# First expert block's rows from one-hot products instead of a gather, and half of its weights split earlier

## What is computed

```python
h2 = modulate(rmsnorm(x, norm_ffn[l]), sh2, sc2)
x = x + gt2[:, None, :] * moe(h2, ...)

def moe(h, router_w, router_bias, w_gate, w_up, w_down):
    scores = jax.nn.sigmoid(jnp.einsum('bsd,de->bse', h, router_w))
    sel = scores + router_bias
    grp = lax.top_k(sel.reshape(B, S, N_GROUPS, per), TOP_K)[0].sum(-1)
    g_idx = jnp.argmax(grp, axis=-1)
    ...
    _, e_idx = lax.top_k(jnp.where(in_grp, sel, -jnp.inf), TOP_K)
    w = jnp.take_along_axis(scores, e_idx, axis=-1)
    w = w / jnp.sum(w, axis=-1, keepdims=True)
    hid = silu(h @ w_gate[e]) * (h @ w_up[e])      # for each chosen expert e
    return sum over chosen e of w[e] * (hid @ w_down[e])
```

## Time and profile before

| what | us |
|---|---|
| median of 3 runs | 2239.13 |
| lowest and highest of these | 2235.25, 2240.95 |
| the profiled execution's own time | 2234.31 |
| its span, from the first to the last instruction | 2232.5 |
| TensorE's granted clock over that span, share of full speed | 0.989 |

### The profile page before, as it was taken

The page is one execution under the profiler, slowest core; times in us unless marked ns, Lnnn a source line. Parts: engine busy times, 40 slices in busy tenths (PEclk is TensorE's granted clock), DMA queues, the critical chain, the costliest instruction groups (busy, mean ns, idle before and its releaser), DMA issues.

```text
span 2232.5 us, 32746 instructions
## 1 busy us (share of the span) xinstructions
PE 2124.1 (95%) x12051; PEld 1703.5 (76%) x12051; DVE 1484.5 (66%) x2695; ACT 1010.4 (45%) x1867; POOL 381.1 (17%) x346
## 2 busy tenths in 40 slices
PE   7999999999899999999999999999998999999996
PEld 4897788787687786777679978888966878677774
DVE  4728766655767876777646487666367688377775
ACT  4523334554565325555435333345445643445551
POOL 2002200000001431444300021000000034124441
PEclk9999999999999999999999999999999999999998
DMA  9332233241325765766542222333222277446653
GB/s 315 95 88 62 81 119 95 77 120 55 89 93 183 267 240 222 276 250 248 189 150 88 81 81 85 102 110 105 77 70 81 81 257 270 201 158 240 244 211 121
DMA packets 196573, 333.71 MB, mean 149 GB/s; under 512 B 30528, under 2 KB 153280, under 8 KB 180416
## 3 DMA queue, kind: packets, MB, share of 16 engines
q1 hardware_dynamic: 169184, 305.33, 40.4%
q0 software_dynamic: 19296, 19.98, 2.8%
q10 hardware_dynamic: 7936, 6.30, 0.9%
HBM read 352.48 MB, written 51.38 MB: 181 GB/s over the span
## 4 chain that ended last, share of the span: by engine, by line
PE 76%; DVE 12%; ACT 5%; issue 3%; DMA 2%; POOL 0%; SPq 0%; POOLq 0%; DVEq 0%; ACTq 0%
PE ps L875 70%; PE ps L873 6%; DVE spare L2089 3%; DVE ring_rounded L2107 2%; ACT WH_rounded L1588 1%; DMA SQKV<-gate_logits 1%; DVE nmax L2344 1%; DVE SC L2717 1%; DMA Y<-y_rows 1%; DVE ps L2341 0%; DVE ssq L2274 0%; POOL M L3059 0%; DVE SC L2367 0%; DVE spare L2092 0%; DVE SQKV L2285 0%
## 5 line engine op out<-in xcount | busy, mean ns | idle before, releaser
L875 PE MATMUL ps<-X_rounded,WH_rounded 128*128 128x512 f32 x768 | 340.0, 443 | 16.4 <-DVE ring_rounded L2107 4.5
L2107 DVE TENSOR_TENSOR ring_rounded<-ring,WH_rounded 128x512 fp32r<-128x512 f32 (+2 forms) x190 | 234.6, 1243 | 132.8 <-ACT WH_rounded L1588 132.4
L875 PE MATMUL ps<-H_rounded,WH_rounded 128*128 128x512 f32 x768 | 301.4, 392 | 3.2 <-DVE SC L2717 3.0
L875 PE MATMUL ps<-X_rounded,ring_rounded 128*128 128x512 f32 x768 | 301.7, 393 | 0.0
L875 PE MATMUL ps<-WH_rounded,X_rounded 128*128 128x256 f32 (+1 forms) x960 | 274.8, 286 | 3.1 <-ACT TM L1800 1.0
L875 PE MATMUL ps<-ring_rounded,X_rounded 128*128 128x256 f32 (+1 forms) x960 | 271.3, 283 | 0.0
L875 PE MATMUL ps<-WH_rounded,H_rounded 128*128 128x256 f32 (+1 forms) x960 | 271.2, 282 | 0.0
L3059 POOL TENSOR_TENSOR M<-M,SC 128x512 f32<-128x512 f32 x48 | 79.5, 1670 | 947.0 <-DVE SC L2717 947.0
L1588 ACT ACTIVATE WH_rounded<-ring 128x512 fp32r<-128x512 f32 (+2 forms) x190 | 195.1, 1036 | 77.0 <-PE ps L875 65.5
L875 PEld LDWEIGHTS ps<-X_rounded,WH_rounded 128*128 128x128 f32 x768 | 144.9, 189 | 69.4 <-issue 27.9
L875 PEld LDWEIGHTS ps<-WH_rounded,X_rounded 128*128 128x128 f32 x960 | 184.4, 192 | 5.3 <-issue 2.4
(11 more groups left out here) (399 smaller groups left out, 4484.0 us busy)
## 6 DMA issues: line engine op xcount, KB each, us to landing
ring<-in_w_in SPq DMA_DIRECT2D x272, 256.0 KB, 4.0
Y<-in_moe_w_down SPq DMA_DIRECT2D x18, 1024.0 KB, 6.8
ring<-in_ada_w SPq DMA_DIRECT2D x64, 256.0 KB, 4.6
ring<-in_w_branch SPq DMA_DIRECT2D x64, 256.0 KB, 5.3
TM<-in_ada_w SPq DMA_DIRECT2D x14, 1024.0 KB, 10.0
DQK<-in_ada_w SPq DMA_DIRECT2D x14, 1024.0 KB, 9.2
ring<-in_moe_w_down SPq DMA_DIRECT2D x14, 1024.0 KB, 5.9
gate_logits<-CM SPq DMA_DIRECT2D x44, 256.0 KB, 2.7
```

Source lines behind the costliest of these rows:

```text
L875: ins = nc.tensor.matmul(o, lhsT, rhs, start=start, stop=stop)
L2107: ins = v.tensor_tensor(low[j][:, at:at + size], ring[:, j, at:at + size], high[i][:, at:at + size].bitcast(F32), ALU.subtract)
```

## The change

**Rows of block 0.** DVE makes four one-hot tiles first_hot (128 tokens by 128 places each, in CM) as soon as it has the ranks: the place's number is compared with the token's rank in expert 0, times whether the token chose it. PE multiplies the token rows h_tok with these, 32 products of 128 columns (two halves, four feature tiles each, summed over four token tiles), straight into banks 2 and 0, where rows_turn(0) put its result. This goes ahead of the find products. gather(0), rows_turn(0) and their place in rows_in go; gather(1) is the first, and gather(2), which writes over h_tok's first tile, waits for rows_used[0], which PE gives behind the products. The stores of h to DRAM stay, as the other blocks are gathered.

**Weights of block 0.** The first two quarters of pair_high(0) go ahead of the sigmoid on ACT, with the wait for the two weight loads; the first two of pair_low(0) go ahead of the router's steps on DVE. The other two quarters stay where all four were. DVE's turn_low(0) now also waits for h_stored, since it writes over a tile of h_tok.

**Products that nobody reads.** warm(13) becomes warm(4); warm(8) and warm(2) go.

```diff
--- before.py
+++ after.py
@@ -549,6 +549,7 @@
...
         onehot = heads(sc[:, 0:2 * S], 2 * NT)
+        first_hot = heads(flat(CM[:, :, :])[:, 2 * S:3 * S], NT)
...
@@ -1438,8 +1439,22 @@
...
                 free(1)
-                warm(13, 5)
+                warm(4, 5)
+                eng.wait_ge(h_copied, p.next(h_copied, 2))
+                alone()
+                for b in (0, 2):
+                    free(b)
+                    alone()
                 eng.wait_ge(routed, p.next(routed, 2))
+                for f in range(2):
+                    for k in range(4):
+                        for t in range(NT):
+                            last = (k, t) == (3, NT - 1)
+                            ins = mm(ps[:, (2, 0)[f], tt(k)], h_tok[t][:, 4 * f + k::NC], first_hot[:, t],
+                                     t == 0, t == NT - 1, last=last)
+                    ins.then_inc(turned[f], p.gives(turned[f]))
+                later(rows_used[0])
+                eng.wait_ge(routed, p.next(routed))
...
                 alone()
                 for n in range(2 * NT):
@@ -1448,15 +1463,13 @@
...
-                eng.wait_ge(h_copied, p.next(h_copied, 2))
-                for b in (0, 1, 3, 4, 5, 6, 7):
+                for b in (1, 3, 4, 5, 6, 7):
...
                     alone()
                 for c in range(NC):
...
-                warm(8, 5)
...
                 def rows_turn(j):
...
@@ -1513,8 +1526,6 @@
...
                     later(expert_used)
...
-                rows_turn(0)
-                warm(2, 5)
                 for j in range(BLOCKS + 1):
...
@@ -1967,6 +1978,24 @@
                 shift(3 * NC, Hc, h_ready)
                 nc.scalar.preload_act_table_set("sigmoid_and_others")
...
+                def pair_high(j, qs=range(4)):
+                    if 0 in qs and SEQ[j] < NE:
+                        for m in range(2):
+                            at = (3 * j + m) % SLOTS
+                            eng.wait_ge(place_loaded[at], p.next(place_loaded[at], 16))
+                    elif 0 in qs:
+                        eng.wait_ge(over_loaded[j % AHEAD], p.next(over_loaded[j % AHEAD], 48))
+                    for q in qs:
+                        act(piece(pair_hi[j % 2], q), piece(pair_w[j % AHEAD], q), ACT.Copy).then_inc(
+                            act_high, p.gives(act_high))
+                for i in (0, 1):
+                    p.mark(place_loaded[i], 16 * (l == 0))
+                for i in ROW_PLACES:
+                    p.mark(place_loaded[i], 16)
+                pair_high(0, range(2))
                 eng.wait_ge(filled[6], p.next(filled[6]))
                 act(scores_T, ps[0:NE, 6], ACT.Sigmoid).then_inc(emptied[6], p.gives(emptied[6]))
...
@@ -1990,23 +2019,7 @@
...
-                def pair_high(j):
-                    if SEQ[j] < NE:
-                        for m in range(2):
-                            at = (3 * j + m) % SLOTS
-                            eng.wait_ge(place_loaded[at], p.next(place_loaded[at], 16))
-                    else:
-                        eng.wait_ge(over_loaded[j % AHEAD], p.next(over_loaded[j % AHEAD], 48))
-                    for q in range(4):
-                        act(piece(pair_hi[j % 2], q), piece(pair_w[j % AHEAD], q), ACT.Copy).then_inc(
-                            act_high, p.gives(act_high))
-                for i in (0, 1):
-                    p.mark(place_loaded[i], 16 * (l == 0))
-                for i in ROW_PLACES:
-                    p.mark(place_loaded[i], 16)
-                pair_high(0)
+                pair_high(0, range(2, 4))
                 turn_copy(0)
                 for j in range(BLOCKS + 1):
...
@@ -2024,7 +2037,7 @@
...
                 eng.wait_ge(routed, p.next(routed, 2))
-                p.mark(routed, 3)
+                p.mark(routed, 4)
...
@@ -2761,6 +2774,16 @@
...
                 p.mark(filled[7])
+                def pair_low(j, qs=range(4)):
+                    for q in qs:
+                        eng.wait_ge(act_high, p.next(act_high))
+                        v.tensor_tensor(piece(pair_lo[j % AHEAD], q), piece(pair_w[j % AHEAD], q),
+                                        piece(pair_hi[j % 2], q).bitcast(F32), ALU.subtract).then_inc(
+                            act_ready, p.gives(act_ready))
+                pair_low(0, range(2))
                 eng.wait_ge(handed[7], p.next(handed[7]))
...
@@ -2842,6 +2865,10 @@
...
                 rank, n_of, extra, upto, first = place_of[:, 1], *(counts[:, k] for k in range(4))
                 eng.wait_ge(emptied[0], p.given(emptied[0]))
+                for t in range(NT):
+                    ins = v.tensor_scalar(first_hot[:, t], iota[:, :], rank[:, t * NE:t * NE + 1],
+                                          whole[:, 0, t * NE:t * NE + 1], ALU.is_equal, ALU.mult)
+                ins.then_inc(routed, p.gives(routed))
                 past, beyond = whole[:, 1], whole[:, 2]
...
@@ -2890,22 +2917,19 @@
...
                 def turn_low(j):
...
+                    if j == 0:
+                        eng.wait_ge(h_stored, p.next(h_stored, 16 * NT))
+                        alone()
+                        eng.wait_ge(act_high, p.next(act_high, 2))
                     for f in range(2):
                         at = slice(4 * f, 4 * f + 4)
-                        eng.wait_ge(act_high, p.next(act_high))
+                        if j:
+                            eng.wait_ge(act_high, p.next(act_high))
                         v.tensor_tensor(rows_lo[j % 2][:, at], bank3((2, 0)[f], 4, P),
...
-                def pair_low(j):
-                    for q in range(4):
-                        eng.wait_ge(act_high, p.next(act_high))
-                        v.tensor_tensor(piece(pair_lo[j % AHEAD], q), piece(pair_w[j % AHEAD], q),
-                                        piece(pair_hi[j % 2], q).bitcast(F32), ALU.subtract).then_inc(
-                            act_ready, p.gives(act_ready))
-                pair_low(0)
+                pair_low(0, range(2, 4))
                 turn_low(0)
...
                 for f in range(2):
@@ -3080,10 +3104,13 @@
...
                 def gather(j):
...
-                    if j >= 2:
+                    if j >= 3:
...
                         alone()
-                    if j >= 3:
+                    if j == 2:
+                        eng.wait_ge(rows_used[0], p.next(rows_used[0]))
+                        alone()
+                    if j >= 4:
...
                         alone()
                     eng.indirect_dma_start(rows_in[j % 3], None, h_dram, bass.IndirectOffsetOnAxis(
@@ -3114,9 +3141,8 @@
...
                 alone()
-                eng.wait_ge(routed, p.next(routed, 5))
+                eng.wait_ge(routed, p.next(routed, 6))
                 alone()
-                gather(0)
                 gather(1)
                 for j in range(BLOCKS + 1):
...```

PE around the places, layer 0, before. CM, SC, M and DVt in the rows are buffers: SC holds the tiles of the places, M block 0's gathered rows; "waits" are semaphores.

```order
L875 MATMUL ps<-lmask,ident 128x256 [waits emptied5,handed5,handed1,emptied1]
L875 MATMUL ps<-lmask,ident 128x256 x12
L875 MATMUL ps<-SC 128x46 [waits routed]
L875 MATMUL ps<-SC 128x46 x7
L875 MATMUL ps<-ident,mod 128x128 [waits handed0,h_copied,emptied0,emptied1,handed1,emptied3,handed3,emptied4,handed4,emptied5,handed5,emptied6,handed6,emptied7,handed7]
L875 MATMUL ps<-ident,mod 128x128 x7
L875 MATMUL ps<-lmask,ident 128x256 [waits handed5,emptied5]
L875 MATMUL ps<-lmask,ident 128x256 x7
L873 MATMUL ps<-ident,M 128x128 [waits rows_gathered0]
L873 MATMUL ps<-ident,M 128x128 x7
```

## The result

The changed kernel takes 2243.81 us (median of 11 runs, 2239.13 to 2251.93) against 2239.13 for the kernel before (11 runs beside them): ratio 1.0029, 95% interval 1.0019 to 1.0039. It is 4 to 9 us slower, where 10 us less were forecast: outside the range, and on the other side of no change. The profiled execution took 2248.29 us, its span 2246.5.

The account below looks back on a forecast made before the run. The prediction took a serial path (router, places, find, gather, turn, split) to bound the seam, with PE waiting on it; 5.4 us in layer 0 plus 5.05 in layer 1, 10.4 off 2239.13, gave 2229 us, range 2223 to 2237.

Parts of the forecast that it names:

- One-hot products: PE, between places and find: 64 records at 0.112 us from start to start, 7.17 us a layer.
- break-even: One-hot products on PE: at 0.195 us a record nothing is gained.
- upper bound: One-hot products on PE: a record's whole duration, 0.277 us, if none overlaps the next, 17.7 us for 64.
- No overlap, the rival: One-hot products: each record ends before the next weights load, 0.277 us a record, 10.6 us slower, 2249.7; chance 0.05.
- The path before: Seam before block 0: PE, though busy, waits on router, places, find, gather, turn, split; unread products run until the gather lands.
- Early weights: ACT waits for block 0's loads, sigmoid 0.83 and 1.15 us late; DVE's two early quarters cost nothing.
- Tiles: Four one-hot tiles on DVE, 0.9 us, hidden behind warm(4) by 0.2 us.
- Find: Find products on PE behind the one-hot products: 16 at full clock take 1.91 us.
- Splits: DVE behind find: two weight quarters instead of four, 2.31 us, then the rows' low halves, 1.30 us.
- The clock, a rival: Half clock over gate products and part of gate_up(0): about 2 us a layer, 2232.7; at worst 2242; chance 0.17.
- block 1's rows were there in time: gather(1), now POOL's first, lands at 874.8; PE wants the rows at 877.7, 2.8 us spare.
- the blocks moved as one: After block 0's start, all ACT, DVE and POOL steps keep their distance to PE.

Follow-up runs that it names:

- contiguous kernel without the early half: Changed kernel with one-hot weights' columns stored next to each other and all four weight quarters split behind the router: 2232.27 us, ratio to before 0.9978.
- the cure: Changed kernel with token rows stored so that the one-hot products' weight columns lie next to each other: 2227.87 us, ratio to before 0.9958.
- products alone: Changed kernel with all four weight quarters of block 0 split behind the router again, one-hot products kept: 2248.95 us, ratio to before 1.0044.

## Why the prediction was wrong, point by point

- **One-hot products: the step that failed.** The forecast took 0.112 us a record from the earlier trace rows, whose weights lie next to each other, and set the step of eight columns aside with the turned tiles of the earlier trace rows, read at the same step at 0.112 each. Turned tiles and f32 products differ in just that: the first start 0.109 us apart at either step, since their load bears it (140 and 188 ns), the second cost double (load 192 and 335 ns). Measured 0.238; 64 records were 8.17 us longer in layer 0 (15.34 for 7.17) and 8.16 in layer 1. Taken from the forecast of -10.4 this gives +5.9; found were +6.5. The break-even that the prediction named, 0.195 a record (its terms give 12.37 / 64 = 0.193), was passed. Its upper bound, 0.277, held the value, but its rival had the wrong mechanism and so too small a chance.
- **No overlap, the rival.** The time came out on its side, not its cause. Contiguous records with new weights on all rows run at 0.113, with 192 ns of load and 277 of product inside. The rule of the Trainium skill that stands with it (TensorE: Matmul & The Clock Gate, "What overlaps and what doesn't") doesn't hold in these rows. The rule that did bear on the change, that on 16-byte lines, the prediction passed over.
- **The path before.** The prediction had PE wait for the gather. The rows had landed 2.5 and 2.4 us before PE turned them; PE was still at warm(8), which the prediction took for a mere filling of that wait. No term of the sum hangs on this, as both leave the path, but the 10.4 us were not the gather's alone.
- **Early weights.** Cost at the sigmoid: forecast 0.83 and 1.15 us, measured 1.68 and 0.67. In layer 0 the later load took 9.9 us from its issue at 836.08 to landing and not 9.1, and ACT began at 846.06; in layer 1 ACT found it there. The cause was right, the landing is worth about a microsecond either way. That DVE's two early quarters cost nothing held.
- **Tiles.** Forecast 0.9 us, measured 1.11 for four. Find: 1.91 forecast, 1.88 measured. Splits: two quarters 2.31 and low halves 1.30 forecast, 2.35 and 1.28 measured.
- **The clock, a rival.** It came in part. The clock fell over the gate products, to 0.51 in layer 0 and for a part in layer 1. They took 3.54 and 2.85 us, but most of that lay beside DVE's split: block 0 started at 882.13, 0.52 us after the low halves (880.33 + 1.28). In layer 1 the half clock went on into block 0 and made gate_up(0) 0.7 us longer, where the rival had 1 to 1.5. The same code had gate products of 2.02 us in one layer and 3.53 in the other of one execution (the contiguous kernel without the early half), so the fall isn't fixed by the code at this place.
- **The sum by steps**, layer 0, against the forecast from the router's first product: sigmoid +0.85, then the products start only 0.77 late (the tiles' 0.2 and the warm products' slack lie in between), products +8.17, behind them +0.40: 42.97 for 33.63. Layer 1: -0.56, +8.16, -0.06: 41.52 for 33.98.
- **What held.** Gather, turning and warm products left the path; block 1's rows were there in time in both layers; the blocks moved as one (in layer 0 PE's products kept their distance from block 0's first one to 0.05 us up to about 1400 us, in layer 1 they keep it too, but for the 0.7 us of gate_up(0)). With contiguous weights the same chain came out at 33.69 and 33.43 us against the forecast's 33.63 and 33.98, and the time 9.4 us below before against 10.4.

## What to carry to other kernels

A price from a nearest row holds only for the same operation with the same access pattern on each operand: before a product's operand gets a step of more than 8 bytes, look for a row of the same product at that step, and don't take a turned tile's for it: compare the weight loads as well, since a longer load can be hidden in one and not in the other. Where an operand is written by an engine that copies it anyhow, let that copy put its columns next to each other; here that cost nothing and turned a loss of 0.3% into a gain of 0.4%. An engine that waits behind a longer step (DVE's 9.13 us here, 1.03 after the cure) is the place for the work that stands behind it. And a wait that a chain puts down to a transfer is checked against its landing: here PE was held by its own unread products.

## What the runs showed of the hardware

- f32 products of 128x128 at full clock, new weights in each record, took 0.113 to 0.125 us a record at steps of 4 and 8 bytes, 0.174 at 12 (weights), and 0.224 to 0.238 at 16 to 32, whichever operand had the step; where both had it 0.119 at 8, 0.180 at 12 and 0.240 at 16 and 32.
- Turned tiles of the same size took 1.03 to 1.05 us for eight at a step of 4 and of 32 bytes, though their weight loads took 140 ns at 4 and 188 at 32.
- After 3.05 to 3.08 us of PE's idle time ahead of block 0 (products alone, both layers; contiguous without the early half, layer 0) the granted clock fell to half over a part of block 0 each time, which cost 1.6 us.
- ScalarE's copy of 512 columns out of PSUM cost the same whether it read them in order or every eighth: two in 1.05 to 1.09 us.
- The later of block 0's two loads of 1 MB landed 6.9 to 10.2 us after its issue over the runs and their layers; a wait on it can move the sigmoid by the difference.
